# Reordering the joints between the blocks of a fused two-block forward kernel

## What is computed

```python
# first block
h = h + rms_norm(moba_attention(rms_norm(h, norm_mix_pre)), norm_mix_post)
u = jnp.square(jax.nn.relu(rms_norm(h, norm_ffn_pre) @ w_up)) @ w_down
h = h + rms_norm(u, norm_ffn_post)
# second block, each half layer l of four
mods = silu(c) @ ada_w[l] + ada_b[l]           # 1024 -> 3072
shift, scale, gate = jnp.split(mods, 3)
h = rms_norm_2(x, gain) * (1 + scale) + shift
x = x + gate * y(h)                            # hgrn2, swiglu, nsa, swiglu
```

## Time and profile before

| what | value |
|---|---|
| median of 3 runs | 1047.74 us (1044.75 to 1048.33) |
| the profiled execution | 1047.76 us |
| its span | 1046.0 us |
| granted TensorE clock, mean | 0.992 of full |
| TensorE busy | 996.8 us, 95% |
| VectorE busy | 741.3 us, 71% |
| ScalarE busy | 513.0 us, 49% |
| GpSimd busy | 127.3 us, 12% |
| DMA, mean | 218 GB/s |

### The profile page before, as it was taken

One profiled execution on the slowest core, in us unless ns is written; L12 is line 12 of the kernel. 1 busy time (PEld: TensorE's weight loads), 2 busy tenths in 40 slices (PEclk: granted clock), 3 DMA queues, 4 the chain that ended last, 5 costly groups with the idle time before them and its releaser, 6 DMA issues.

```text
span 1046.0 us, 15096 instructions
## 1 busy us (share of the span) xinstructions
PE 996.8 (95%) x5644; PEld 817.7 (78%) x5644; DVE 741.3 (71%) x996; ACT 513.0 (49%) x669; POOL 127.3 (12%) x147
## 2 busy tenths in 40 slices
PE   8998999999988999888999999989999989999998
PEld 6777778888866887776788888768868767888886
DVE  4777777766757779987787786888837776454454
ACT  5745374454445675652444343445367625434341
POOL 1000000000001001760510000013911210000000
PEclk9999999999999999999899999999999999999999
DMA  9993379797744976006698989556340337565541
GB/s 352 360 376 142 121 268 353 274 367 246 278 164 131 395 277 209 2 18 255 184 384 315 333 293 332 210 200 210 103 162 3 101 101 226 173 212 173 201 141 59
DMA packets 113650, 227.65 MB, mean 218 GB/s; under 512 B 5024, under 2 KB 58544, under 8 KB 113600
## 3 DMA queue, kind: packets, MB, share of 16 engines
q1 hardware_dynamic: 112048, 222.34, 59.8%
q0 software_dynamic: 1408, 4.54, 1.6%
q10 hardware_dynamic: 144, 0.10, 0.0%
HBM read 225.90 MB, written 1.06 MB: 217 GB/s over the span
## 4 chain that ended last, share of the span: by engine, by line
PE 81%; DVE 10%; ACT 3%; DMA 2%; issue 2%; SPq 1%; POOL 1%; DVEq 0%; ACTq 0%; PEldq 0%
PE psum L1757 76%; DMA raw<-in_attn_w_qkv 1%; DVE wlo L1162 1%; PE psum L2331 1%; DVE arena L1217 1%; PE psum L1775 1%; DMA adaw<-in_ada_w 1%; PE psum L2186 1%; DVE arena L1263 1%; ACT arena L753 1%; DVE res L1268 1%; PE psum L2059 1%; ACT whi L742 1%; DVE gain_b L1467 1%; DVE arena L1467 1%
## 5 line engine op out<-in xcount | busy, mean ns | idle before, releaser
L1162 DVE TENSOR_TENSOR wlo<-raw,whi 128x2048 fp32r<-128x2048 f32 (+1 forms) x160 | 316.8, 1997 | 145.7 <-ACT whi L742 145.6
L1757 PE MATMUL psum<-whi,xhi 128*128 128x512 f32 x880 | 350.6, 398 | 5.6 <-DVE xlo L1226 3.0
L1757 PE MATMUL psum<-whi,xlo 128*128 128x512 f32 x880 | 345.0, 392 | 0.0
L742 ACT CAST whi<-raw 128x2048 fp32r<-128x2048 f32 (+1 forms) x160 | 267.2, 1676 | 158.7 <-PE psum L1757 119.5
L1757 PE MATMUL psum<-wlo,xhi 128*128 128x512 f32 x880 | 343.7, 392 | 0.0
L1757 PEld LDWEIGHTS psum<-whi,xhi 128*128 128x128 f32 x880 | 166.8, 190 | 43.4 <-issue 7.1
L1757 PEld LDWEIGHTS psum<-whi,xlo 128*128 128x128 f32 x880 | 166.5, 189 | 35.6
L1757 PEld LDWEIGHTS psum<-wlo,xhi 128*128 128x128 f32 x880 | 167.0, 190 | 33.3
L1178 DVE SCALAR_TENSOR_TENSOR adaw<-adaw,crow 128x1024 f32<-128x1024 f32 x112 | 132.2, 1224 | 2.4 <-DMA adaw<-in_ada_w 2.3
L1757 PE MATMUL psum<-whi,hhi 128*128 128x512 f32 x304 | 119.4, 393 | 4.7 <-DVE wlo L1162 2.5
L1757 PE MATMUL psum<-whi,hlo 128*128 128x512 f32 x304 | 118.4, 389 | 0.0
(11 more groups left out here) (265 smaller groups left out, 953.5 us busy)
## 6 DMA issues: line engine op xcount, KB each, us to landing
adaw<-in_ada_w SPq DMA_DIRECT2D x48, 1024.0 KB, 7.4
raw<-in_ffn_w_in SPq DMA_DIRECT2D x88, 512.0 KB
raw<-in_ffn_w_out SPq DMA_DIRECT2D x44, 512.0 KB
raw<-in_w_up SPq DMA_DIRECT2D x16, 1024.0 KB
raw<-in_w_down SPq DMA_DIRECT2D x16, 1024.0 KB
raw<-in_hgrn_w_in SPq DMA_DIRECT2D x16, 1024.0 KB
raw<-in_attn_w_qkv SPq DMA_DIRECT2D x10, 1024.0 KB
adaw<-in_kv_ada_w SPq DMA_DIRECT2D x8, 1024.0 KB, 8.0
```

Source lines behind the costliest of these rows:

```text
L742: sc.copy(whi[:, s, 0:width], raw[:, s, 0:width]).then_inc(hi_ready[s], 1)
L1162: ve.tensor_tensor(wlo[:, s, 0:width], raw[:, s, 0:width], whi[:, s, 0:width].bitcast(F32), ALU.subtract).then_inc(lo_ready[s], 1)
L1757: return te.matmul(dst, lhsT, rhs, start=start, stop=stop, skip_group_check=open_)
```

## The change

It touches the ends and starts of all blocks, on all five engines.

1. The zero matmuls go; the first products of a feed-forward start the banks (`begin`).
2. The second tile's transposes inside the first tile's products move from `k == 2` to `k == 1`.
3. End of the first feed-forward: the last hidden values' second half goes to `xhi` and `xlo`; the last slot is split in two halves of columns (`columns`), and `last_down1` uses them in order; modulation columns `mods(0)` are made before the last step; the second tile's residual stands between the affine pairs of the first (`normed_begin`, `post_added`, `normed_end`); the slot splits of the HGRN projections come after the norm on ScalarE; fillers go from 14 to 8 and from 4 to 6.
4. Ten half blocks of modulation weights, by the table `HIN_ADA`, are loaded and reduced in the HGRN projections instead of eight; the A_HOUT block is among them.
5. The last head's scores go to banks 0 and 1 and wait for one GpSimd product less; in the HGRN output the second half comes before the first with `second` between.
6. At the joints into the second and third feed-forwards (`joint`) the splits of slot 1 stand before the scaling, and half of the second tile's sum moves to GpSimd (`tile_added`, `p_add`), ahead of its norm step; at the end of the second feed-forward as well.
7. End of the second feed-forward: the last slots' parts go to the upper halves of the buffers (`split_upper`, `w0=1024`), before the last hidden values.
8. NSA: two of four key copies go to VectorE, the hidden product to bank 6, its transposes one unit later, `mods(3)` earlier.
9. In the NSA output the next norm's transposes stand within the products (`next_norm=5`).

The diff, cut to its core; all parts that sit in the sections of one engine follow in the order SyncE, GpSimd, ScalarE, VectorE, TensorE:

```diff
+HIN_ADA = {1: {0: 0, 1: 1, 2: 2}, 2: {0: 3, 1: 4}, 3: {0: 5, 1: 6, 2: 7}, 4: {0: 8, 1: 9}}
...
+            return w[:, 3, :].rearrange("p (k n) -> p k n", k=2)[:, :, 512 * f:512 * f + 512]
...
+        def score_bank(h):
+            return 2 if h < HH - 1 else 0
...
-                    if t and s < 2:
-                        ada_block(A_HIN + t - 1, s)
+                    if s in HIN_ADA.get(t, ()):
+                        n = HIN_ADA[t][s]
+                        ada_block(A_HIN + n // 2, n % 2)
...
-            for half in range(2):
-                ada_block(A_HOUT, half)
...
+            def tile_added(k):
+
+                pool.wait_ge(h_gate, k - 1)
+                gp.tensor_tensor(res[:, 1, 0:512], res[:, 1, 0:512], y[:, 1, 0:512], ALU.add).then_inc(p_add, 1)
...
-            pool.wait_ge(ada_used[0], A_HOUT)
-            pool.wait_ge(ada_used[1], A_HOUT)
+            pool.wait_ge(ada_used[0], A_HOUT + 1)
+            pool.wait_ge(ada_used[1], A_HOUT + 1)
...
-            norms(3)
+            norm(3, 0)
+            tile_added(2)
+            norm(3, 1)
...
-            norms(5)
+            norm(5, 0)
+            tile_added(4)
+            norm(5, 1)
...
+            def split_upper(s, n):
+
+                act.wait_ge(raw_full[s], 32 * n + 32)
+                sc.copy(whi[:, s, 1024:2048], raw[:, s, 0:1024]).then_inc(hi_ready[s], 1)
...
-                    if last and b == 1:
-                        act.wait_ge(used[3], t + Q_FF1)
-                    sc.copy(hhi[:, 2 * b:2 * b + 2, :], sq[:, 2 * b:2 * b + 2, :]).then_inc(h_hi, 1)
-                split(3, t + Q_FF1)
+                    dst = xhi[:, 0:2, :] if last and b == 1 else hhi[:, 2 * b:2 * b + 2, :]
+                    sc.copy(dst, sq[:, 2 * b:2 * b + 2, :]).then_inc(h_hi, 1)
+                if last:
+                    n = t + Q_FF1
+                    act.wait_ge(raw_full[3], 32 * n + 32)
+                    act.wait_ge(used[3], n)
+                    for f in range(2):
+                        sc.copy(columns(whi, f), columns(raw, f)).then_inc(hi_ready[3] if f else half_hi, 1)
+                else:
+                    split(3, t + Q_FF1)
...
-            norm_high(2, 0)
+            norm_high(2, 0, stop=2)
+            norm_square(2, 1)
+            norm_high(2, 0, start=2)
+            norm_high(2, 1)
             split(2, Q_HIN)
-            norm_square(2, 1)
-            norm_high(2, 1)
             split(3, Q_HIN)
...
-                if not last:
+                if last:
+                    split(0, t + (q0 + 1), 1024)
+                    split(1, t + (q0 + 1), 1024)
+                elif end:
+                    split_upper(2, t + q0)
+                    split_upper(3, t + q0)
+                else:
                     split(1, t + (q0 + 1), nxt)
                     split(2, t + q0, 1024)
...
-                if not last:
+                if last:
+                    return
+                if end:
+                    split(1, t + (q0 + 1), nxt)
+                else:
                     split(3, t + q0, 1024)
...
+                ve.tensor_tensor(wlo[:, s, 1024:2048], raw[:, s, 0:1024], whi[:, s, 1024:2048].bitcast(F32), ALU.subtract).then_inc(lo_ready[s], 1)
...
+            def normed_begin(k, j):
+
+                affine_pair(k, j, 0, 0)
+                affine_pair(k, j, 0, 1)
+                low(k, 0, 0)
+
+            def normed_end(k, j, begun=1):
+
+                if begun == 1:
+                    low(k, 0, 1)
+                affine_pair(k, j, 0, 2)
+                affine_pair(k, j, 0, 3)
+                low(k, 0, 2)
+                low(k, 0, 3)
...
+            def post_added(k, i):
+
+                v.wait_ge(p_rstd, 2 * k + i + 1)
+                ve.scalar_tensor_tensor(res[:, i, :], y[:, i, :], stat[:, 38 + i:39 + i], res[:, i, :],
+                                        ALU.mult, ALU.add).then_inc(p_res, 1)
...
+            def gated_first(k):
+
+                gated_half(k, 1, 0, done=h_gate)
...
-            with v.Fori(5, N_FF1) as t:
+            with v.Fori(5, N_FF1 - 1) as t:
                 mlp1(t, t + A_FF1)
             mods(0, VR["mix2"], 6)
+            mlp1(N_FF1 - 1, N_FF1 - 1 + A_FF1, last=True)
             residual(1, 0)
             norm_scale(2, 0)
-            normed_tile(2, 2, 0)
-            residual(1, 1)
+            gained(1, 1)
+            normed_begin(2, 2)
+            post_added(1, 1)
+            normed_end(2, 2)
             norm_scale(2, 1)
             normed_tile(2, 2, 1)
             split(2, Q_HIN)
             split(3, Q_HIN)
+            mods(1, VR["ffn2"], 12)
...
+                    ada(A_HIN + n // 2, n % 2)
...
                         split(1, Q_HIN + t + 1)
-                        ada(A_HIN + t, 1)
+                        hin_ada(t, 1)
                     elif t < N_HIN - 1:
+                        hin_ada(t, 2)
                         split(3, Q_HIN + t + 1)
...
-            mods(1, VR["ffn2"], 12)
-            ada(A_HOUT, 0)
-            ada(A_HOUT, 1)
...
-            def up_starts(q0, k, j, m=None):
-                residual(j - 1, 0)
-                if m is not None:
-                    split_one(q0, 0)
-                    norm_scale(j, 0)
-                    gated_half(j - 1, 1, 0)
-                else:
-                    gated_half(j - 1, 1, 0)
-                    norm_scale(j, 0)
-                normed_tile(k, j, 0)
-                if m is not None:
-                    split_one(q0, 1)
-                added(1, 0, 1)
+            def joint(k, j):
+
+                normed_begin(k, j)
                 gated_half(j - 1, 1, 1)
+                low(k, 0, 1)
+                v.wait_ge(p_add, j - 2)
                 added(1, 1, 2).then_inc(p_res, 1)
+                normed_end(k, j, 2)
                 norm_scale(j, 1)
                 normed_tile(k, j, 1)
-            up_starts(Q_F2A, 3, 3, A_HOUT)
+
+            residual(2, 0)
+            split_one(Q_F2A, 0)
+            split_one(Q_F2A, 1)
+            norm_scale(3, 0)
+            gated_first(2)
+            joint(3, 3)
...
-                if not last:
+                if last:
+                    return
+                if end:
+                    split(1, t + (q0 + 1), nxt)
+                else:
                     split(3, t + q0, 1024)
...
-            mlp2(N_FF2 - 1, Q_F2A, HT_F2A, 0, M_END - 1, end=True)
             mods("kv", VR["kvn"], M_L3, 16)
             mods(2, VR["mix2"] + 8, M_L3)
+            mlp2(N_FF2 - 1, Q_F2A, HT_F2A, 0, M_END - 1, end=True)
             residual(3, 0)
-            for f in range(2):
-                gated_half(3, 1, f)
+            gated_first(3)
+            gated_half(3, 1, 1)
             norm_scale(4, 0)
-            normed_tile(4, 4, 0)
-            added(1).then_inc(p_res, 1)
-            split(2, Q_NQ)
+            v.wait_ge(p_add, 2)
+            added(1, 1, 2).then_inc(p_res, 1)
+            normed_begin(4, 4)
...
+            for b in range(2, 4):
+                v.wait_ge(k_["kT"], b + 1)
+                ve.tensor_copy(nkT.rearrange("p b h t -> p (b h) t")[:, 2 * b:2 * b + 2, :],
+                               psum[:, 4 + b, :].rearrange("p (k t) -> p k t", k=2)).then_inc(k_["kTd"], 1)
...
@@ -1735,10 +1837,12 @@
             turn_low(2, 2)
             turn_low(2, 3)
             split(3, Q_NOUT)
-            mods(3, VR["ffn2"] + 8, M_END)
             split(0, Q_F2B)
+            residual(4, 0)
             split(1, Q_F2B)
-            up_starts(Q_F2B, 6, 5)
+            norm_scale(5, 0)
+            gated_first(4)
+            joint(6, 5)
...
+                    if turns is not None and k == 1:
                         norm(turns, 1)
...
+                    if i == (0 if s == 0 and second is not None else 1):
                         ins.then_inc(used[s], 1)
...
                     ins.then_inc(used[0], 1)
+                elif second is not None:
+                    part(0, 1)
+                    second()
+                    part(0, 0)
                 else:
                     part(0, 0)
-                    if second is not None:
-                        second()
                     part(0, 1)
                 if late is not None:
...
+            def last_down1(n, low):
+
+                def part(i, f, s):
+                    for k in range(2):
+                        h = [x[:, k, i * P:(i + 1) * P] for x in ((hhi, hlo) if s == 2 else (xhi, xlo))]
+                        ins = three(psum[:, 2 * i + f, :], h[0], h[1], s, k * D + f * 512, 512, False, s == 3 and k == 1, True)
+                    return ins
+                pe.wait_ge(h_lo, low + 1)
+                item_ready(2, n)
+                part(0, 0, 2)
+                part(0, 1, 2)
+                pe.wait_ge(h_lo, low + 2)
+                pe.wait_ge(half_lo, 4)
+                part(0, 0, 3).then_inc(acc_half, 1)
+                item_ready(3, n)
+                part(0, 1, 3).then_inc(acc_done, 1)
+                part(1, 0, 2)
```

(20 more changed lines are left out.)

121 lines of the change are left out of this document (66 added, 55 removed).

## The result

The changed kernel takes 1023.47 us (median of 4 runs, 1023.22 to 1023.87), the kernel before 1047.58 beside it: ratio 0.9775, 95% interval 0.9757 to 0.9794. The forecast was 1025.8, with a range of 1018 to 1034. The profiled execution took 1023.87 us with a span of 1022.1, 23.9 less than before.

What follows compares the result with a forecast made beforehand. The prediction took TensorE as the bound, with idle time and lower clock at four joints between blocks; its terms summed to -22.0 us, from 1047.8 to 1025.8 us, range 1018 to 1034.

Steps and rivals of the forecast that it cites:

- The bound: Whole kernel: TensorE, busy 95% of the span, sets the time; its long idle stretches lie at four joints between blocks.
- the second step: Second feed-forward, second step: a plain gain of 0.96 us from dropping one set of four zero matmuls.
- The first two joints: First feed-forward's end through the HGRN projections to the first head: net gain shrinks to 2.5 us, bounds -7.9 to +0.
- First norm, heads, attention: Three terms: first norm joint +0.7 us, end of the heads -1.2 (0 to -2.1), attention -1.1 (0 to -1.4).
- Opened accumulators: Feed-forward starts: dropping three sets of four zero matmuls saves 0.96 us each, -2.9 us.
- End of the first feed-forward: Joint into the HGRN projections: last products run without their waits, second tile's transposes wait 0.4 us; -7.9 us.
- HGRN projections: Before the first head: VectorE works without rest, gate functions come 3.8 us earlier, cold start +0.6; 3.1 of 7.9 is left.
- the rival in which the stage keeps the gain: HGRN projections: loads land early enough and VectorE's idle time is usable, another 5.4 us go, 1020.4 us; chance 0.13.
- The sign named for it: Ahead of the heads: a wait of 3 to 5 us on VectorE before the second head's exponents would show the forecast right.
- HGRN output into feed-forward: Joint into the second feed-forward: residual no longer behind two half-blocks; GpSimd's one-column step costs +0.9; sum -6.0 us (-4 to -8).
- The two other joints: End of the second feed-forward -5.5 us (-3.5 to -6.5); attention output into the last feed-forward -3.5 (-2 to -4.5).
- the sign named for them: After the first joint: TensorE's waits for the scaled activations under 3 us in total would show the forecast right.
- GpSimd holding VectorE at every joint: Rival at three joints: GpSimd's half sums meet VectorE's low-half subtractions, each loses 1 to 2 us more, 1030; chance 0.07.

## Why the prediction held, step by step

- **The bound.** TensorE is the bound everywhere but at the joints: the lead changes only in stretches for which the prediction has a term. In one of them, the second step, it moves the other way.
- **The sum.** The span fell by 23.9 us, 22.0 were forecast. The first two joints gave 4.4 us (8.1 less 3.7) instead of 2.5, and the second step cost 0.5 instead of giving 0.96. These two misses, 1.9 and 1.5 us, nearly cancel, and that is luck; the other terms are off by 0.5 us or less each.
- **First norm, heads, attention.** 0.5 for 0.7, 1.3 for 1.2, 0.6 for 1.1: within their bounds.
- **Opened accumulators.** The mechanism held, the term was mis-sized: 1.2 us a set, not 0.96, since the row of the four matmuls doesn't hold the gap at either end. I had taken a duration where the distance between its neighbours was the price.
- **End of the first feed-forward.** 8.1 for 7.9. The last products run without a wait, and the second tile's transposes wait 0.2 us, where 0.4 was forecast.
- **HGRN projections.** The step that VectorE works without rest to the first head held, and the run without the sums of two half blocks shows it as the bound. Two sizes inside were off. The gate functions, and the split behind them, came 7.1 us earlier (371.88 to 364.76), not 3.8, as the loads slipped less than I had worked out: ScalarE's copy ahead of the gate functions waited 1.65 us for one. Against it the cold start cost 1.5 us (3.68 us for ten matmuls, 2.13 before), not 0.6. So 3.7 were given back, not 5.4: between the forecast and the rival in which the stage keeps the gain. The sign named for it came nearly as told: TensorE waits 3.47 us for VectorE ahead of the first head (some 4 were forecast), and ScalarE's exponents that follow wait 3.83. The 4.7 us taken for four sums of 1.22 should have been 4.9, which changes nothing here.
- **HGRN output into feed-forward.** 6.3 for 6.0. GpSimd's step grew to 1.03 us, as the earlier trace rows said it would, and the run with the subtraction out of its way shows the cause. The half sum took 1.29 for 1.3. What the prediction didn't see is that this gain and the loss in the projections are largely one and the same: the block's two halves give 3.9 us here and cost 3.7 there. Nor did it see that one half in each place costs nothing in either.
- **The second step.** The prediction has here a plain gain of 0.96 for the zero matmuls, and no wait; the lead fell by 0.5. VectorE sums two pieces of 1.3 us ahead of the gated values, and its split there waits 2.0 us for a copy of ScalarE that waits 3.7 for its load:

```profile
507.04 1.91 ACT L761 CAST whi<-raw 128x2048 fp32r<-128x2048 f32 x1 [3.72 <-DMA raw<-in_ffn_w_in]
...
508.99 2.30 DVE L1201 TENSOR_TENSOR wlo<-raw,whi 128x2048 fp32r<-128x2048 f32 x1 [2.01 <-ACT whi L761]
```

In the kernel before that copy waited 1.20 us for its load, at 517.25, and VectorE's split not at all. The copy comes 10.2 us earlier now, TensorE is 12.7 ahead: the load has not kept up, and a wait of 1.49 came in. The run with the sums behind the product shows that they stood in the way: the wait is gone.
- **The two other joints.** 6.0 for 5.5 and 4.0 for 3.5. But the sign named for them failed: the scaled activations' waits after the first joint are 4.4 us, not under 3. The first tile's are 1.3 to 1.4 at each of the three joints. The second tile's are 0.2 or nothing, and the matmuls behind them no longer run at the lower clock, which brought a part of the gain.
- **GpSimd holding VectorE at every joint** didn't come: with the half sums back on VectorE the kernel isn't faster, and no half sum takes over 2 us.

## What to carry to other kernels

When an edit lets an engine reach the next stage sooner, price it together with that stage's longest row of work without a pause: here nearly half of the joint's gain was taken by 43 us of VectorE work whose start hung on a load. Work moved from one stage to another is only cheaper if the place that it goes to is idle. Here each place had room for one half block: the projections took nine as cheaply as eight, the joint covered one, and the tenth in the projections or the second at the joint cost nearly 4 us. And the matmuls behind a wait of 3 to 4 us on TensorE took 0.7 to 1.9 us longer, while waits of 1.3 us left the clock full. So the first aim at a joint is a short wait, not none.

## What the runs showed of the hardware

The lower clock after a wait isn't told by the wait's length alone. At the first head ten matmuls took 2.12 to 2.17 us behind waits of 1.30, 1.31, 1.75 and 2.58 us, but 2.79 to 3.87 behind waits of 2.11, 2.54, 3.29, 3.31, 3.37, 3.40, 3.42 and 3.47. In the run with the half sums back on VectorE, a wait of 1.42 at the last joint was followed by the lower clock (0.63 in the window shown), and one of 1.44 at the joint into the second feed-forward wasn't (1.00 from 488 to 492). The Trainium skill, TensorE: Matmul & The Clock Gate, section "What's actually happening", says that the same kernel can start with different numbers of slow matmuls from one run to another; that is told of a kernel's start. The executions here differ in the same manner: among those of the kernel before, one of 1050.16 us has a mean granted clock of 0.987 and one of 1045.73 has 0.995. That both have one cause isn't shown.

VectorE and GpSimd hold each other in both directions. GpSimd's one-column step took 1.03 us beside a subtraction of two SBUF operands and 0.18 without; VectorE's scaling of 1024 columns, with one SBUF operand, took 1.69 us beside GpSimd's half sum and 0.75 elsewhere. The second the prediction hadn't expected. The Trainium skill, SBUF — State Buffer, section "Who interferes with whom", has it: a `tensor_scalar` can run in a mode that takes the port which VectorE shares with GpSimd, and who issues first keeps it. The trace agrees: GpSimd's sum had begun 0.12 us earlier.
